# Updating the inverse's transpose by products instead of transposing at every level

## The reference, cut to what matters

```
lmat = where(strict lower, einsum(k_beta, kc) * decay, 0)
tmat = triangular_solve(eye + lmat, eye, lower, unit_diagonal)     # the inverse
u    = einsum(tmat, v_beta)
w    = einsum(tmat, k_beta * exp(gc))
...                                                                 # then the state is updated chunk by chunk
```

## Time and profile before

| what | value |
|---|---|
| median of 3 runs | 2997.94 us |
| profiled execution | 2997.94 us |
| its span, first to last instruction | 2996.6 us |
| mean granted TensorE clock | 0.981 |
| TensorE busy | 2857.2 us, 95% |
| VectorE, ScalarE, GpSimd busy | 45%, 37%, 44% |
| HBM traffic, mean | 96 GB/s |

### The profile page before, as it was taken

How to read it: one execution, slowest core, us unless ns; L and a number is a source line. 1 busy time by engine, 2 the same in 40 slices (tenths; PEclk the granted TensorE clock), 3 DMA queues, 4 the chain that set the end, 5 groups by cost and what they waited for, 6 DMA issues and landing times.

```text
span 2996.6 us, 40926 instructions
## 1 busy us (share of the span) xinstructions
PE 2857.2 (95%) x16292; PEld 2360.0 (79%) x16292; DVE 1345.2 (45%) x2490; ACT 1118.3 (37%) x1885; POOL 1322.6 (44%) x884
## 2 busy tenths in 40 slices
PE   7889998999999899989999899999999999999999
PEld 6576777988888786778888787888778878888787
DVE  4447643132121475632121356775442368665422
ACT  3342553553322443543332344232333343323332
POOL 4253246774444451344444344444634433436343
PEclk9999999999999999999999999999999999999999
DMA  6843214553323323122323221111222221212222
GB/s 225 312 135 117 86 44 132 176 159 103 98 92 98 120 67 123 58 71 92 98 92 99 68 99 67 57 57 57 85 71 92 80 87 52 66 54 73 78 71 85
DMA packets 81357, 291.67 MB, mean 97 GB/s; under 512 B 9104, under 2 KB 9488, under 8 KB 80784
## 3 DMA queue, kind: packets, MB, share of 16 engines
q1 hardware_dynamic: 81168, 289.06, 29.3%
HBM read 286.93 MB, written 2.10 MB: 96 GB/s over the span
## 4 chain that ended last, share of the span: by engine, by line
PE 83%; DVE 8%; POOL 3%; issue 3%; ACT 2%; DMA 0%; SPq 0%; POOLq 0%; DVEq 0%; ACTq 0%
PE ps L595 63%; PE ps L568 6%; PE ps L738 3%; PE ps L759 2%; POOL t L2791 2%; PE ps L623 2%; DVE ps L2166 1%; PE ps L990 1%; PE ps L927 1%; PE ps L1001 1%; PE ps L863 1%; DVE t L1990 1%; POOL t L2811 1%; PE ps L1168 1%; DVE t L2456 1%
## 5 line engine op out<-in xcount | busy, mean ns | idle before, releaser
L595 PE MATMUL ps<-t,t 128*128 128x512 f32 (+3 forms) x9936 | 2216.3, 381 | 35.6 <-POOL t L2791 16.3
L595 PEld LDWEIGHTS ps<-t,t 128*128 128x128 f32 x9936 | 1785.5, 190 | 381.5 <-issue 42.2
L2791 POOL TENSOR_TENSOR t<-t,t 128x1024 fp32r<-128x1024 f32 (+3 forms) x444 | 1041.6, 2349 | 1097.9 <-ACT t L1301 1043.2
L1301 ACT ACTIVATE t<-t 128x1024 fp32r<-128x1024 f32 (+3 forms) x444 | 458.1, 1035 | 901.3 <-PE ps L595 853.4
L568 PE MATMUL ps<-t,t 128*128 128x128 f32 (+2 forms) x1676 | 247.3, 285 | 58.1 <-DVE t L1990 20.6
L568 PEld LDWEIGHTS ps<-t,t 128*128 128x128 f32 (+2 forms) x1676 | 198.5, 145 | 108.4 <-issue 23.7
L2269 DVE TENSOR_TENSOR ps<-ps,t 128x512 f32<-128x512 f32 (+1 forms) x96 | 57.2, 605 | 341.9 <-ACT t L1576 341.9
L2282 DVE TENSOR_TENSOR t<-ps,t 128x512 f32<-128x512 f32 x60 | 40.9, 691 | 217.7 <-PE ps L595 217.6
L2811 POOL TENSOR_TENSOR t<-t,t 128x4 f32<-128x4 f32 (+2 forms) x93 | 85.6, 921 | 76.7 <-DVE t L1956 39.2
L2166 DVE SCALAR_TENSOR_TENSOR ps<-t,t,ps 128x512 f32<-128x512 f32 (+1 forms) x174 | 116.1, 667 | 6.8 <-ACT ps L1504 0.9
L738 PE MATMUL ps<-t,t 96*128 96x384 f32 (+1 forms) x320 | 109.5, 466 | 3.9 <-DVE t L2034 1.5
(11 more groups left out here) (258 smaller groups left out, 2470.2 us busy)
## 6 DMA issues: line engine op xcount, KB each, us to landing
t<-in_wbig SPq DMA_DIRECT2D x412, 512.0 KB, 3.5
t<-in_wmod SPq DMA_DIRECT2D x96, 512.0 KB, 6.8
t<-in_wbig SPq DMA_DIRECT2D x16, 416.0 KB, 3.1
t<-in_wbig SPq DMA_DIRECT2D x14, 256.0 KB, 2.6
t<-in_wbig SPq DMA_DIRECT2D x8, 332.0 KB, 2.9
t<-in_wbig SPq DMA_DIRECT2D x6, 384.0 KB, 3.0
t<-in_x SPq DMA_DIRECT2D x1, 2048.0 KB, 8.0
out<-t SPq DMA_DIRECT2D x1, 2048.0 KB, 6.6
```

The lines of the kernel that those rows point to most:

```text
L595: m = p.matmul(out, lhs, rhs, start=kk == 0 and n == 0, stop=kk == tiles - 1 and n == 2)
L1301: a.activation(c.hi(w), c.raw(w), ACT.Copy).then_inc(w_hi.h, w_hi.up(("cut", w)))
L2791: g.tensor_tensor(c.lo(w), c.raw(w), c.hi(w).bitcast(F32), ALU.subtract).then_inc(w_lo.h, w_lo.up(("cut", w)))
```

## The change

The transpose TT is no longer made anew at each level. After level 0, T is transposed once (d10) and copied to TT by ScalarE. At each of levels 1 to 5 TensorE then makes two products from X: f (X as weights, odd blocks of TT moving), which VectorE subtracts from TT, and g (TT as weights, even blocks of X moving), which VectorE subtracts from T. Level 6 stays as it was. VectorE waits for g, then subtracts f from TT, then g from T. Since X is now full weights at every level, GpSimd sets its odd blocks to zero before every level, once g of the level before has read X, and VectorE's write of X waits for this. f and g each hold a PSUM bank; e holds one alone.

```diff
@@ pe_program, chunk
-        yield
+        B = bank(side, ("d10", q), (act, ("TT", q)), held=True)
+        P.wait_ge(dve, ("T", q, 0))
+        turn4(B, T, ("d10", q))
+        yield
+        done(("d10", q))
         for s in range(1, 7):
...
             B = bank(side, ("e", q, s), (dve, ("X", q, s)), held=True)
             P.wait_ge(act, ("LT", q))
+            P.wait_ge(act, ("TT", q))
             P.wait_ge(dve, ("T", q, s - 1))
...
-            B = bank(side, ("tt", q, s - 1), (act, ("TT", q, s - 1)), held=True)
-            turn4(B, T, ("tt", q, s - 1))
-            yield
-            done(("e", q, s), ("tt", q, s - 1))
-            B = bank(side, ("f", q, s), (dve, ("T", q, s) if s < 6 else ("TT", q, s)), held=True)
+            yield
+            done(("e", q, s))
+            B = bank(side, ("f", q, s), (dve, ("TT", q, s)), held=True)
             P.wait_ge(dve, ("X", q, s))
-            P.wait_ge(act, ("TT", q, s - 1))
+            if s > 1:
+                P.wait_ge(dve, ("TT", q, s - 1))
             for h in range(4):
-                if s < 6:
-                    m = p.matmul(dense(B, h), TT[:, h, :], half(X, h, 0), start=True, stop=True)
-                else:
-                    m = p.matmul(dense(B, h), X[:, h, :], half(TT, h, 1), start=True, stop=True)
+                m = p.matmul(dense(B, h), X[:, h, :], half(TT, h, 1), start=True, stop=True)
             m.then_inc(product.h, product.up(("f", q, s)))
-            yield
-            done(("f", q, s))
+            if s < 6:
+                C = bank(side, ("g", q, s), (dve, ("T", q, s)), held=True)
+                for h in range(4):
+                    m = p.matmul(dense(C, h), TT[:, h, :], half(X, h, 0), start=True, stop=True)
+                m.then_inc(product.h, product.up(("g", q, s)))
+            yield
+            done(("f", q, s), *([("g", q, s)] if s < 6 else []))
@@ act_program, chunk
-        for s in range(6):
...
-            A.wait_ge(turned, ("tt", q, s))
-            a.activation(changed(TT), changed(h4(c.bank(("tt", q, s)))), ACT.Copy).then_inc(
-                act.h, act.up(("TT", q, s)))
+        A.wait_ge(turned, ("d10", q))
+        a.activation(TT, h4(c.bank(("d10", q))), ACT.Copy).then_inc(act.h, act.up(("TT", q)))
@@ dve_program, chunk
-            if l == 6:
-                V.wait_ge(pool, ("X0", q))
+            V.wait_ge(pool, ("X0", q, l))
...
-            V.wait_ge(product, ("f", q, l))
+            V.wait_ge(product, ("f", q, l) if l == 6 else ("g", q, l))
+            v.tensor_tensor(parts4(TT, 1), parts4(TT, 1), dense(c.bank(("f", q, l))), ALU.subtract).then_inc(
+                dve.h, dve.up(("TT", q, l)))
             if l < 6:
-                V.wait_ge(turned, ("tt", q, l - 1))
-                v.tensor_tensor(parts4(T, 0), parts4(T, 0), dense(c.bank(("f", q, l))), ALU.subtract).then_inc(
+                v.tensor_tensor(parts4(T, 0), parts4(T, 0), dense(c.bank(("g", q, l))), ALU.subtract).then_inc(
                     dve.h, dve.up(("T", q, l)))
...
@@ pool_program, chunk
-            if l == 6:
-                G.wait_ge(product, ("f", q, l - 1))
-                g.memset(X.rearrange("p h (t b) -> p h t b", t=2)[:, :, 1, :], 0.0).then_inc(
-                    pool.h, pool.up(("X0", q)))
+            w = 1 << l
+            if l == 1:
+                G.wait_ge(dve, ("T", q, 0))
+            else:
+                G.wait_ge(product, ("g", q, l - 1))
+            g.memset(X.rearrange("p h (g t b) -> p h g t b", t=2, b=w)[:, :, :, 1, :], 0.0).then_inc(
+                pool.h, pool.up(("X0", q, l)))
```

More of the change, by code:

```diff
@@ L1640, in chunk @@
         yield
-        for s in range(6):
-            w = 1 << s
-            def changed(ap):
-                return ap.rearrange("p h (g t b) -> p h g t b", t=2, b=w)[:, :, :, 1, :] if s else ap
+        A.wait_ge(turned, ("d10", q))
+        a.activation(TT, h4(c.bank(("d10", q))), ACT.Copy).then_inc(act.h, act.up(("TT", q)))
+        for _ in range(6):
             yield
-            A.wait_ge(turned, ("tt", q, s))
-            a.activation(changed(TT), changed(h4(c.bank(("tt", q, s)))), ACT.Copy).then_inc(
-                act.h, act.up(("TT", q, s)))
             yield
@@ L2372, in chunk @@
             yield
-            V.wait_ge(product, ("f", q, l))
+            V.wait_ge(product, ("f", q, l) if l == 6 else ("g", q, l))
+            v.tensor_tensor(parts4(TT, 1), parts4(TT, 1), dense(c.bank(("f", q, l))), ALU.subtract).then_inc(
+                dve.h, dve.up(("TT", q, l)))
             if l < 6:
-                V.wait_ge(turned, ("tt", q, l - 1))
-                v.tensor_tensor(parts4(T, 0), parts4(T, 0), dense(c.bank(("f", q, l))), ALU.subtract).then_inc(
+                v.tensor_tensor(parts4(T, 0), parts4(T, 0), dense(c.bank(("g", q, l))), ALU.subtract).then_inc(
                     dve.h, dve.up(("T", q, l)))
-            else:
-                v.tensor_tensor(parts4(TT, 1), parts4(TT, 1), dense(c.bank(("f", q, l))), ALU.subtract).then_inc(
-                    dve.h, dve.up(("TT", q, l)))
+                V.wait_ge(dve, ("T", q, l))
         yield
```

## The result

The changed kernel takes 3022.15 us (median of 4 runs, 3021.54 to 3027.17), the kernel before 2999.12 us in the same comparison. The ratio is 1.0077, with a 95% interval of 1.0059 to 1.0094: slower, by 23 us. The forecast was 3014.5 us, with a range to 3021. The direction was right, and the time is 1 us outside the range. Of the 7.7 us between the time and the forecast, 1.2 us are no growth: the kernel before takes 2999.12 us here, and the forecast had started from 2997.94 us.

The account below looks back on a forecast made before the run. TensorE was taken as the bound: +17.2 us net for products less transposes, -1.6 for swallowed waits, +0.8 for banks, +16.4 us on 2997.94 us, rounded to 3014.5 us. The range was 3009 to 3021 us.

Parts of the forecast that it names:

- What bounds the kernel, and the sign: Whole kernel: TensorE, busy in 95% of the span, sets the time; slower was given 95%, faster 2%.
- ScalarE's freed copies: Delta-rule chunks: six copies of TT per chunk become one; no TensorE wait names them, so nothing for the time.
- The rival of the price by columns: TensorE's products and transposes: columns moved set the price, so -17.2 us, ending at 2980.7 us; chance 2%.
- The price of the products, 0.84 us: TensorE, levels 1 to 5: each added group f of four heads' products costs 0.84 us, 4.2 us per chunk.
- The price of the transposes, 0.41 us: TensorE: each group of four transposes costs 0.41 us; net 5 groups fewer save 2.05 us per chunk.
- The old waits: TensorE's e waiting for T's subtraction, 3.2 us idle in all: 0.4 us swallowed at each of four places, -1.6 us.
- The banks: PSUM rotation, chunks 1 and 3: transposes d4 wait for d2's bank until VectorE writes qn, +0.4 us per layer, +0.8 us.
- GpSimd: 0: Zeroing X's odd half at each level, 40 more of at least 0.30 us, is covered by 3.8 us: costs 0.
- d10: the step that failed: Before the levels: one added group of four transposes per chunk, priced at 0.41 us, with no wait for T counted.
- the slack of X: VectorE's write of X before the product that reads it: 0.28 us at its tightest place becomes 0.38 us.
- VectorE becomes the bound at more levels: Rival: the added subtractions make T late by 0.33 us at all 40 levels, +13 us more, 3028 us; chance 11%.

Follow-up runs that it names:

- the control: The changed kernel, unaltered, run again on the same chip beside three other runs: ratio 1.0098 to the kernel before, median 3026.61 us.

## Why the prediction was right and wrong

**What bounds the kernel, and the sign.** Right. TensorE's program sets the end, the sum below leaves nothing for ScalarE's freed copies, and a product costs twice a transposition. The rival of the price by columns, the only one that ended faster, would have needed the opposite.

**The price of the products, 0.84 us: too low.** Adding up the distances from start to start over the first stretch of the run with zeroing at two levels (clock at 1.00, all products present), f and g take 37.3 us where f took 19.2 us in the kernel before: 18.1 us for 20 groups, 0.91 us each. With d10 later it is 17.9 us, with the products added to the kernel before 0.89 us by the same sum (0.87 us from the growth of the whole stretch). A group that starts behind another one is followed 0.86 to 0.89 us later, as the earlier trace rows had it once (0.87 us); I took this for the upper bound, though every added group stands in such a pair; as the value it would have given 1.2 us of the difference. The measured price lies above it for two reasons that the starts show: g is followed after 0.89 us on the mean, and f, which is now always followed by g, costs a little more than alone (0.853 us on the mean against 0.834 us; before, nine of the twenty groups of L1001 were followed after only 0.81 us, and my rows had none of these). **+2.7 us** (36.3 against 33.6).

**The price of the transposes, 0.41 us.** Measured 0.395 us by the same sum (7.9 us for 20 groups in a stretch, 15.8 us against 16.4): **+0.6 us**.

**The old waits: -1.6 us forecast.** All 3.2 us went: **-1.6 us**. TensorE now comes to e after T at all four places.

**The banks: +0.8 us forecast.** No wait of d4 is in the trace: **-0.8 us**. I had pushed back TensorE alone, by 0.84 us. In the control d4 starts at 1876.79 us, 2.2 us later after the start of the stretch than before, and qn is ready at 1876.72 us, just in time.

**GpSimd: 0.** Right, with the zeroing near the lower bound of its price (0.32 us against 0.30).

**d10: the step that failed.** I counted its transposes and put its wait for T at nothing, without asking: it waits 0.64 and 1.53 us in each layer, 4.3 us in all. A second, small miss is the slack of X, for which I had worked out that 0.38 us remain: f waits 0.2 us for it in each layer. With small gaps these are the control's whole idle time in the stretches, **+4.8 us**. Moving d10 back gives 4.7 us. That is close to 4.8 us but not the same sum: the idle time falls by 3.9 us, since waits of 0.2 us at an e and at an f are left in each layer, and the matmuls take 0.7 us less. My rival "VectorE becomes the bound at more levels" looked at the T of the levels. Leaving it out was right for T at the levels; the place was before the first.

The sum: 16.4 + 2.7 + 0.6 - 1.6 - 0.8 + 4.8 = 22.1 us, and the control's stretches have grown by 22.0 us. The timed 23 us of the first comparison agree with it within their interval (18 to 28 us). In executions in which the clock falls behind the wait, 1.4 us per layer come on top; which of the timed ones did is not known.

**What stays open.** The timed runs of one kernel spread over 3 to 12 us, those of the control over 14.5 us. The starts of the first delta stretch in the ten traces alone lie 11.7 us apart, so much of this comes before the change; I did not look for its cause. The control's interval, 23 to 35 us of growth, lies above the 22.0 us of its own trace: two of its five executions took 3034 and 3036 us, and no trace shows where. No version tried is faster than the kernel before and does its whole computation. Of those that keep TT up to date by products the best, with d10 one step later, is 0.7% slower. The product that keeps TT up to date costs 0.87 to 0.91 us of TensorE, the transposition that it replaces 0.39 us.

## What to carry to other kernels

Price small matmuls by instructions, from start to start, in the neighbourhood in which the new ones will stand, and read how many instructions the profile records for each kind: here a plain float32 product has two and a transposition one, so "fewer columns" was more work. For every operation that is moved to an earlier step, look up when its input is written in the trace of before, and subtract. An empty step in an order written by hand can be the time that another engine needs.

## What the hardware showed that I had not expected

A single wait of TensorE of 1.53 us in an otherwise full stretch came with 3.4 us at the 1.2 GHz level in both layers of one execution and in neither of another of the same kernel. Over all traces: of the eight stretches with a wait of 1.4 to 1.5 us for T (the changed kernel twice, with zeroing at two levels, without the subtractions) three have such a dip, one of them in the second layer alone of the run without the subtractions; of the two with 2.3 us both have it; of the ten without a wait for d10's T (the longest other wait is 1.27 us) none has. So the dip goes with the wait and does not always follow it; what decides is not shown. A wait can then cost more than its length: the early transposition in the kernel before grew the stretches by 8.1 us, where its new waits are 3.0 us per layer less some 0.7 us of old ones, 4.6 us in all. The remaining 3.5 us are longer busy time of TensorE, which has the two dips in it.
